# Moving nine weight sums behind the heads' scaling and the gating in VectorE's program (second layer of a fused block)

## The chip, the cores and the metric

The kernel runs on one core of a Trainium2 chip. The metric is the device time of one execution in microseconds (us), given as the median of several runs. Five engines take part: TensorE (PE in the profile; PEld is its loading of weights), VectorE (DVE), ScalarE (ACT), GpSimd (POOL) and SyncE (SP), which here only issues DMAs. Each works through its own program in order, and they wait for each other through semaphores.

## The reference, cut to what matters

The program is a stack of four layers. The one that is touched is the second, a neighbourhood attention over 512 tokens and 256 context tokens, with 32 heads of 64:

```
q, k, v, z = jnp.split(u @ w_in, 4, axis=-1)
q = rms_norm(q.reshape(bsz, n, NA_HEADS, NA_DH), qn_g)   # each head scaled by 1/rms
k = rms_norm(k.reshape(bsz, n, NA_HEADS, NA_DH), kn_g)
...
s = q_r . k_band * scale + bias, masked to the window;  s_ctx = q_r . k_ctx * scale
p = softmax(concat([s, s_ctx]))
o = p_band @ v_band + p_ctx @ v_ctx
out = (o * silu(z)) @ w_out                               # the gating
```

All is float32. The product `u @ w_in` is not computed as it stands, but by a scheme with seven products in the place of eight: the 1024 x 1024 piece of weights that belongs to one kind (k, q, v or z) of one group of heads is cut into quarters b11, b12, b21, b22, and the seven products use sums of quarters of the tokens and of the weights. The sums of the tokens exist once for the layer; the sums of the weights are made by VectorE for each piece ("chunk") anew, four of them, each a subtraction of 128 x 1024 elements:

```
t1 = b12 - b11      (n = 1)
t2 = b22 - t1       (n = 2)
t3 = b22 - b12      (n = 3)
t4 = t2 - b21       (n = 4)
```

## The kernel before, in words

The class `NearMixer` works on four groups of eight heads. The attention of a group is cut into 16 turns, one for a pair of heads and a quarter of the tokens. I number the turns of a group 0 to 15. Beside the attention of one group, TensorE computes the projections of the next group, so the turns of the groups 0, 1 and 2 carry projection products and the weight sums of the next group.

In a turn, TensorE does in this order: the scores (L1560, L1564, L1568), at times a transposition of freshly scaled heads (L1546), projection products (L1511, here four products of four matmuls; each matmul shows as two rows in the trace), the transposition of the softmax weights (L1577) ahead of the last three matmuls, and the attention's outputs (L1592). The products of a chunk come in the order `ORDER = (1, 2, 6, 5, 3, 7, 4)`; product 5 reads t1, product 6 reads t2, product 7 reads t3, product 4 reads t4. For the first step of a chunk TensorE waits for the sum with `pe.wait_ge(self.ts, 4 * b + {6: 2, 7: 3, 4: 4}[p])`. Before the outputs it waits for the gating of the turn before: `pe.wait_ge(self.gy, i)`.

VectorE's program of a turn, in `vector`, is: the maxima of the scores (L1826, L1834, L1839), the early parts (`add_parts`, which adds the products' results from PSUM, L1778 to L1795), the sums of squares of new heads (`sum_squares`, L1870), the softmax weights (`weights`, L1844, L1849, L1855), the held weight sums, the scaling of new heads (`evacuate`, L1881), the gating of the turn before (`gate`, L1863), and the late parts. GpSimd computes the factors 1/rms of the heads between the sums of squares and the scaling, with two small operations per tile of heads, an addition (L1702) and a power (L1704); the scaling waits for them.

A weight sum becomes due behind the part of a certain product. Where that part is an early one, most sums are not made at once but put into the list `self.held` and made later in the turn by `held_sums`; those that become due at a late part are made there. The weight sums are L1732 (t1), L1736 (t2), L1738 (t3) and L1742 (t4), all in `weight_sum`. SyncE loads the next quarters when the products and the third sum of the chunk before are done.

Of the kernel before, what the change touches and what calls it, by code (L numbers as in the profile page):

```python
# [1259 lines left out]
class NearMixer:  # L1260
# [557 lines left out]
    def vector(self, dve):  # L1818
# [3 lines left out]
        def maxima(i):  # L1822
            g, p, n = self.unit(i)
            dve.wait_ge(self.sc, 2 * i + 2)
            ctx = s.psS[:, 0:2, :].rearrange("p k (r x) -> p k r x", r=ROWS)[:, :, :, 0:32]
            nc.vector.tensor_reduce(self.m_ctx, ctx, mybir.AxisListType.XY, ALU.max).then_inc(self.cm, 1)  # L1826
            if n == 0:
                dve.wait_ge(self.bias_in[p], 64 * (g + 1))
            off = 16 - 16 * n + 8 * self.band[n]
            for k in range(2):  # L1830
                slot = s.bias[:, 2 * p + k, :]
                bias = bass.AP(slot.tensor, slot.offset + BANK - 1 - off, [slot.ap[0], [-64, ROWS], [-1, 32]])
                sc = self.scores_of(k)[:, :, 32:]
                nc.vector.tensor_tensor_reduce(  # L1834
                    out=sc, in0=sc, in1=bias, scale=1.0, scalar=-3.0e38, op0=ALU.add, op1=ALU.max,
                    accum_out=self.m_all[k]).then_inc(self.bi, 1)
                dve.wait_ge(self.bi, 2 * i + k + 1)
                dve.wait_ge(self.cm, i + 1)
                nc.vector.tensor_scalar(self.nm[i % 2][k], self.m_all[k], self.m_ctx[:, k:k + 1], -1.0, ALU.max,  # L1839
                                        ALU.mult).then_inc(self.mx, 1)  # L1840

        def weights(i):
            dve.wait_ge(self.ex, 2 * i + 2)
            nc.vector.reciprocal(self.rr, self.r[i % 2]).then_inc(self.rc, 1)  # L1844
            dve.wait_ge(self.rc, i + 1)
            n = self.unit(i)[2]
            if self.odd(n):
                for k in range(2):
                    nc.vector.tensor_scalar(s.e[:, k, BANK:], s.e[:, k, BANK // 2:BANK // 2 + DH], self.rr[:, k:k + 1], 0.5,  # L1849
                                            ALU.mult, ALU.mult).then_inc(self.tails, 1)  # L1850
            for k in range(2):
                e = s.e[:, k, 0:BANK]
                if self.odd(n):
                    dve.wait_ge(self.tails, 2 * self.odd_before(i) + k + 1)
                nc.vector.tensor_scalar(e, e, self.rr[:, k:k + 1], 0.5, ALU.mult, ALU.mult).then_inc(self.wt, 1)  # L1855

        def gate(i):
            g, p, n = self.unit(i)
            if n == 0:
                dve.wait_ge(self.zdone, 4 * g + (0, 2, 1, 3)[p] + 1)  # L1860
            dve.wait_ge(self.o, i + 1)
            cols = slice(n * P, (n + 1) * P)
            nc.vector.tensor_tensor(s.yT[:, g * 4 + p, cols], s.psO[:, 0:P], s.z[:, p, cols], ALU.mult).then_inc(self.gy, 1)  # L1863

        def sum_squares(g, kind, t, f):
            if kind == "z":
                return
            j = self.heads_index(g, kind, t)
            dve.wait_ge(self.sq, f + 1)
            nc.vector.reduce_sum(self.ss[:, j % 2, :], s.squares[f % 2].rearrange(view, h=HG), AX_X).then_inc(self.red, 1)  # L1870

        def evacuate(g, kind, t, f):
            if kind == "z":
                dve.wait_ge(self.sq, f + 1)
                z = s.z[:, t, :]
                nc.vector.scalar_tensor_tensor(z, s.squares[f % 2], 1.0, z, ALU.add, ALU.mult).then_inc(self.zdone, 1)
                return
            j = self.heads_index(g, kind, t)
            dve.wait_ge(self.rstd, j + 1)
            x = s.raw[:, j % 4, :].rearrange(view, h=HG)  # L1880
            nc.vector.tensor_tensor(x, x, spread(self.rs[:, j % 2, :], DH), ALU.mult).then_inc(self.evac, 1)  # L1881
# [8 lines left out]
        def out_part(q):  # L1890
            n, t = self.tiles[q]
            dve.wait_ge(self.pm, q + 1)
            if q == 0:
                dve.wait_ge(self.gate_in, 16)
                dve.wait_ge(self.old_in, 16 * LT)
            else:
                dve.wait_ge(self.pa, q)
            out_gate(s.psP[:, q % 4, :], n, t, self.pg, self.pa, q)
# [10 lines left out]
        def held_sums():  # L1909
            for b, n in self.held:  # L1910
                self.weight_sum(dve, b, n)
            self.held = []

        self.held = []
        for i in self.turns():
            lead = i + self.LEAD_TURNS
            if i >= 0:
                maxima(i)
            self.add_parts(dve, i, True)
            if i < 0:  # L1920
                held_sums()
            if lead in (1, 2):
                for t in range(2):
                    self.norm.vector_evacuate(dve, 2 * lead + t)
                self.norm.half_sums(dve, lead)
            for tile in self.finish[i]:
                sum_squares(*tile)
            if i >= 0:
                weights(i)
            if i >= 0:  # L1930
                held_sums()
            for tile in self.finish[i]:
                evacuate(*tile)
            if i >= 1:
                gate(i - 1)
            self.add_parts(dve, i, False)
            for q in self.out_ended(i - 1):
                out_part(q)
# [2165 lines left out]
```

## Time and profile before

| | us |
|---|---|
| median of 3 runs | 3019.38 (3019.23 to 3020.89) |
| the profiled execution | 3023.39 |
| span of its trace, first to last instruction | 3021.6 |
| PE busy in the span | 2917.1 (97%) |
| VectorE busy | 1500.2 (50%) |
| ScalarE busy | 796.2 (26%) |
| GpSimd busy | 456.1 (15%) |
| stretch of groups 0 to 2 (1440 to 1930 us): PE busy of 490.0 | 472.9 |
| the same stretch: VectorE busy | 306.9 |
| mean granted clock of TensorE | 0.986 of full speed |

Times in the trace are counted from the start of the span. In the timeline a row gives start, duration, engine, line, operation and what was idle just before it, with the instruction that ended the idle time. Instructions of one engine overlap a little at their ends, so that the next one on VectorE starts up to 0.1 us ahead of the end of the one before.

### The profile page before, as it was taken

The page shows a single profiled execution, that of the slowest core. Times are in us where ns is not written, and L with a number is a line of the kernel's source. Part 1 is how long each engine was busy: PE and PEld are TensorE (multiplying, and loading weights), DVE is VectorE, ACT ScalarE, POOL GpSimd, SP SyncE. Part 2 cuts the span into 40 slices and gives each one's busy share as a digit, 9 for nine tenths or more (in the row PEclk, how much of TensorE's full clock was granted, in tenths as well). Part 3 has the DMA queues.
Part 4 walks back from the last instruction along what each step waited for, and adds up shares of the span by engine and source line. Part 5 has one row for each costly group of instructions (what it writes and reads, how often), then busy time and mean ns, then how long its engine had stood idle before and what let it go on. Part 6 is the DMA issues. An engine that isn't in the chain of part 4 may idle for free. (4 is left out here: it accounts for less than half of the span.)

```text
span 3021.6 us, 38719 instructions
## 1 busy us (share of the span) xinstructions
PE 2917.1 (97%) x14883; PEld 1845.4 (61%) x14883; DVE 1500.2 (50%) x3557; ACT 796.2 (26%) x2061; POOL 456.1 (15%) x753
## 2 busy tenths in 40 slices
PE   5999999999999999999999999998999999999999
PEld 2435555555555554588787887753788887544454
DVE  2334545645545443646656666443455656344441
ACT  1113323323333322212323233221322222021230
POOL 0221321312213000120201112000001111011100
PEclk8999999999999999999999999999999999899999
DMA  7340000100012201321121211502421110040101
GB/s 252 118 160 30 29 28 29 56 28 29 29 40 86 97 1 25 124 72 50 49 78 43 71 50 50 181 1 70 127 57 29 29 57 29 1 140 3 56 1 56
DMA packets 137006, 185.65 MB, mean 61 GB/s; under 512 B 22236, under 2 KB 90364, under 8 KB 134772
## 3 DMA queue, kind: packets, MB, share of 16 engines
q1 hardware_dynamic: 135624, 183.09, 19.1%
q8 instruction: 119, 1.95, 0.3%
q14 instruction: 63, 0.52, 0.1%
q10 hardware_dynamic: 1200, 0.09, 0.0%
HBM read 173.49 MB, written 9.67 MB: 61 GB/s over the span
## 5 line engine op out<-in xcount | busy, mean ns | idle before, releaser
L493 PE MATMUL a_psP<-f_place,a_uT 128*128 128x512 f32 x768 | 351.0, 603 | 7.9 <-DMA f_place<-a_w_in 7.9
L493 PE MATMUL a_psP<-a_w,a_uT 128*128 128x512 f32 x768 | 349.2, 599 | 0.0
L753 DVE TENSOR_REDUCE a_small<-a_psS 128x1 f32<-128x768 f32 (+1 forms) x192 | 140.7, 774 | 401.8 <-PE a_psS L521 401.8
L493 PEld LDWEIGHTS a_psP<-f_place,a_uT 128*128 128x128 f32 x768 | 140.7, 192 | 167.3 <-issue 167.3
L493 PEld LDWEIGHTS a_psP<-a_w,a_uT 128*128 128x128 f32 x768 | 139.8, 191 | 158.0 <-issue 158.0
L1511 PE MATMUL b_psP<-n_body,b_uT 128*128 128x256 f32 x768 | 184.1, 382 | 1.3 <-DVE b_raw L1789 0.5
L648 ACT ACTIVATE a_e<-a_psS,a_small 128x768 f32<-128x768 f32 (+1 forms) x192 | 144.0, 754 | 139.0 <-DVE a_small L753 138.6
L1511 PEld LDWEIGHTS b_psP<-n_body,b_uT 128*128 128x128 f32 x768 | 142.8, 192 | 23.0 <-issue 2.8
L655 ACT COPY n_body<-a_psS 128x768 f32<-128x768 f32 (+1 forms) x96 | 63.1, 657 | 311.2 <-PE a_psS L530 311.2
L543 PEld LDWEIGHTS a_psO<-a_v,n_body 128*128 128x128 f32 x896 | 115.1, 192 | 45.9 <-issue 45.9
L1826 DVE TENSOR_REDUCE b_small<-b_psS 128x2 f32<-128x512 f32 x64 | 44.3, 691 | 189.0 <-PE b_psS L1568 189.0
L1663 ACT ACTIVATE n_body<-b_psS,b_small 128x512 f32<-128x512 f32 x128 | 86.8, 683 | 186.5 <-DVE b_small L1839 184.5
L2420 PE MATMUL d_ps<-d_uT,d_w 128*128 128x264 f32 x512 | 125.3, 395 | 0.0
L1670 ACT COPY n_body<-b_psS 128x512 f32<-128x512 f32 x128 | 68.7, 589 | 210.8 <-PE b_psS L1577 210.8
L1511 PE MATMUL b_psP<-b_wt,n_body 128*128 128x256 f32 x512 | 120.4, 382 | 3.1 <-DVE b_wt L1736 3.1
L521 PE MATMUL a_psS<-n_body 64*128 64x256 f32 (+1 forms) x640 | 122.4, 492 | 0.0
L2420 PE MATMUL d_ps<-d_uT,f_place 128*128 128x264 f32 x512 | 121.8, 389 | 0.0
L723 POOL TENSOR_TENSOR a_small<-a_small,a_eps_sum 128x1 f32<-128x1 f32 x96 | 18.3, 191 | 650.2 <-ACT n_body L659 650.2
L543 PE MATMUL a_psO<-a_v,n_body 128*128 128x128 f32 x896 | 115.5, 275 | 0.0
L1511 PEld LDWEIGHTS b_psP<-b_wt,n_body 128*128 128x128 f32 x512 | 95.0, 190 | 20.0 <-issue 5.6
L2420 PEld LDWEIGHTS d_ps<-d_uT,d_w 128*128 128x128 f32 x512 | 96.3, 195 | 15.3
L2420 PEld LDWEIGHTS d_ps<-d_uT,f_place 128*128 128x128 f32 x512 | 94.3, 190 | 15.3 <-issue 0.4
(495 smaller groups left out, 5182.8 us busy)
## 6 DMA issues: line engine op xcount, KB each, us to landing
n_body<-b_w_in SPq DMA_DIRECT2D x49, 512.0 KB, 3.7
f_place<-a_w_in SPq DMA_DIRECT2D x8, 2048.0 KB, 8.9
a_w<-a_w_in SPq DMA_DIRECT2D x8, 2048.0 KB, 9.0
a_yT<-mod_w SPq DMA_DIRECT2D x8, 1536.0 KB, 8.4
a_yT<-mod_w SPq DMA_DIRECT2D x8, 1024.0 KB, 17.8
f_place<-bias_table SPq DMA_DIRECT2D x64, 128.0 KB
f_place<-a_w_in SPq DMA_DIRECT2D x16, 512.0 KB, 6.9
d_w<-a_w_in SPq DMA_DIRECT2D x16, 512.0 KB, 6.9
```

Source lines behind the costliest of these rows:

```text
L493: ins = nc.tensor.matmul(s.psP[:, x % 2, :], s.uT[:, a, t * P:(t + 1) * P], w[:, a, :], start=(a == 0), stop=(a == KD - 1))
L521: ins = nc.tensor.matmul(self.score_banks(k, keys)[:, a:b], s.qT[rows, h, t * P:(t + 1) * P], s.kT[rows, g % 2, h, keys.start + a:keys.sta ...
L543: ins = nc.tensor.matmul(s.psO[:, 0:P], s.pT[:, k * P:(k + 1) * P], s.v[:, g % 2, keys.start // P + k, h * P:(h + 1) * P], start=(k == 0), ...
L648: nc.scalar.activation(s.e[:, k, 0:n], self.score_banks(k, keys), ACT.Exp, bias=self.nm[i % 2][:, k:k + 1], accum_out=self.r[i % 4][:, k:k ...
L655: nc.scalar.copy(s.pT[:, 0:n], self.score_banks(0, keys)).then_inc(self.wTr, 1)
L723: nc.gpsimd.tensor_tensor(self.c[b], self.oss[b], s.eps_sum[:, :], ALU.add).then_inc(self.order_o, 1)
L753: nc.vector.tensor_reduce(self.nm[i % 2][:, k:k + 1], self.score_banks(k, keys), AX_X, ALU.max, negate=True).then_inc(self.mx, 1)
L1511: ins = nc.tensor.matmul(out, lhsT, rhs, start=(a == 0), stop=(a == 3))
L1663: nc.scalar.activation(s.e[:, k, 0:BANK].rearrange("p (b r c) -> p r b c", b=8, c=8), s.psS[:, k, :].rearrange("p (r b c) -> p r b c", b=8 ...
L1670: nc.scalar.copy(s.e[:, k, 0:BANK], s.psS[:, k, :]).then_inc(self.wTr, 1)
L1826: nc.vector.tensor_reduce(self.m_ctx, ctx, mybir.AxisListType.XY, ALU.max).then_inc(self.cm, 1)
L2420: ins = nc.tensor.matmul(ps[:, 3 + x % 2, 0:n], s.w[h % 2][:, b, i, :], s.uT[:, b, half * n:(half + 1) * n], start=(b == 0), stop=(b == KD ...
```

## The change

`held_sums()` is called behind the gating and no longer ahead of the heads' scaling, for turns 0 and up. The turns ahead of the attention (`i < 0`) keep their own call.

```diff
@@ vector @@
                 sum_squares(*tile)
             if i >= 0:
                 weights(i)
-            if i >= 0:
-                held_sums()
             for tile in self.finish[i]:
                 evacuate(*tile)
             if i >= 1:
                 gate(i - 1)
+            if i >= 0:
+                held_sums()
             self.add_parts(dve, i, False)
```

A sum is held at this point in only three turns of a group, and in the groups 0, 1 and 2 alone: t4 of the q chunk in turn 8, t1 of the v chunk in turn 10, t3 of the v chunk in turn 11. Nine instructions move; all engines but VectorE keep their programs. All three turns also scale two tiles of heads.

VectorE, turn 8 of group 0 (L1855 the last of the softmax weights, L1742 the sum t4, L1881 the heads' scaling, L1863 the gating, L1789 the first late part), before with - and after with +:

```order
 L1849 TENSOR_SCALAR n_body<-n_body,b_small 128x64 x2
 L1855 TENSOR_SCALAR n_body<-n_body,b_small 128x512 x2
+L1881 TENSOR_TENSOR b_raw<-b_raw,b_small 128x512 x2
+L1863 TENSOR_TENSOR b_yT<-b_psO,b_z 128x128
 L1742 TENSOR_TENSOR b_wt<-b_wt,n_body 128x1024
-L1881 TENSOR_TENSOR b_raw<-b_raw,b_small 128x512 x2
-L1863 TENSOR_TENSOR b_yT<-b_psO,b_z 128x128
 L1789 TENSOR_TENSOR b_raw<-b_raw,b_psP 128x256
 L1791 TENSOR_TENSOR b_raw<-b_raw,b_psP 128x256
```

The sum t4 has moved past three instructions, two of which wait for GpSimd.

VectorE, turn 11 of group 0 (L1738 is the sum t3, L1783 a late part, behind which t4 of the same chunk, L1742, is made at once); turn 10 looks the same with L1732 (t1) in the sum's place:

```order
 L1849 TENSOR_SCALAR n_body<-n_body,b_small 128x64 x2
 L1855 TENSOR_SCALAR n_body<-n_body,b_small 128x512 x2
+L1881 TENSOR_TENSOR b_raw<-b_raw,b_small 128x512 x2
+L1863 TENSOR_TENSOR b_yT<-b_psO,b_z 128x128
 L1738 TENSOR_TENSOR n_body<-n_body,b_yT 128x4x256
-L1881 TENSOR_TENSOR b_raw<-b_raw,b_small 128x512 x2
-L1863 TENSOR_TENSOR b_yT<-b_psO,b_z 128x128
 L1783 TENSOR_TENSOR b_yT<-b_yT,b_psP 128x256
 L1742 TENSOR_TENSOR b_wt<-b_wt,n_body 128x1024
```

Here too the scaling and the gating now stand directly behind the softmax weights, and the sum ahead of the late parts.

## Rows read from the trace of the kernel before

**Rows 1.** The page, part 1: engine, busy us, share of the span, instructions.
```profile
PE 2917.1 (97%) x14883; PEld 1845.4 (61%) x14883; DVE 1500.2 (50%) x3557; ACT 796.2 (26%) x2061; POOL 456.1 (15%) x753
```

**Rows 2.** Waits of PE, 1440 to 1930 us: total us, times, longest.
```profile
PE b_psO L1592 <- DVE b_yT L1863: 13.1, 14, 1.9
PE b_psP L1511 <- DVE b_wt L1742: 4.0, 3, 1.3
```

**Rows 3.** Timeline of VectorE, turn 8 of group 0: start, us, instruction, idle before.
```profile
1459.80 0.88 DVE L1855 TENSOR_SCALAR n_body<-n_body,b_small 128x512 f32<-128x512 f32 x2
1460.59 1.22 DVE L1742 TENSOR_TENSOR b_wt<-b_wt,n_body 128x1024 f32<-128x1024 f32 x1
1461.72 0.69 DVE L1881 TENSOR_TENSOR b_raw<-b_raw,b_small 128x512 f32<-128x512 f32 x1
1464.22 0.69 DVE L1881 TENSOR_TENSOR b_raw<-b_raw,b_small 128x512 f32<-128x512 f32 x1 [1.81 <-POOL b_small L1704]
1464.83 0.28 DVE L1863 TENSOR_TENSOR b_yT<-b_psO,b_z 128x128 f32<-128x128 f32 x1
```

**Rows 4.** Timeline of PE, turn 8 of group 0.
```profile
1461.96 0.67 PE L1511 MATMUL b_psP<-b_wt,b_uT 128*128 128x256 f32 x2 [1.35 <-DVE b_wt L1742]
...
1465.17 1.09 PE L1592 MATMUL b_psO<-n_body,b_v 128*64 128x128 f32 x16 [0.37 <-DVE b_yT L1863]
```

**Rows 5.** Timeline of GpSimd, turn 8 of group 0: the second tile's addition.
```profile
1460.72 1.75 POOL L1702 TENSOR_TENSOR b_small<-b_small 128x8 f32<-128x8 f32 x1
```

**Rows 6.** Timeline of VectorE, turn 6 of group 1, which has no held sum.
```profile
1620.48 0.88 DVE L1855 TENSOR_SCALAR n_body<-n_body,b_small 128x512 f32<-128x512 f32 x2
1621.48 0.69 DVE L1881 TENSOR_TENSOR b_raw<-b_raw,b_small 128x512 f32<-128x512 f32 x1
1623.70 0.69 DVE L1881 TENSOR_TENSOR b_raw<-b_raw,b_small 128x512 f32<-128x512 f32 x1 [1.53 <-POOL b_small L1704]
```

**Rows 7.** Timeline of GpSimd, turn 6 of group 1: the second tile's addition.
```profile
1621.41 0.20 POOL L1702 TENSOR_TENSOR b_small<-b_small 128x8 f32<-128x8 f32 x1
```

**Rows 8.** Timeline of VectorE, turn 11 of group 0.
```profile
1490.41 0.69 DVE L1826 TENSOR_REDUCE b_small<-b_psS 128x2 f32<-128x512 f32 x1
...
1494.88 0.87 DVE L1855 TENSOR_SCALAR n_body<-n_body,b_small 128x512 f32<-128x512 f32 x2
...
1499.90 0.28 DVE L1863 TENSOR_TENSOR b_yT<-b_psO,b_z 128x128 f32<-128x128 f32 x1
```

**Rows 9.** Timeline of PE, end of turn 10 to end of turn 11, group 0.
```profile
1488.16 1.09 PE L1592 MATMUL b_psO<-n_body,b_v 128*64 128x128 f32 x16 [1.93 <-DVE b_yT L1863]
...
1492.49 1.67 PE L1511 MATMUL b_psP<-b_wt,n_body 128*128 128x256 f32 x7
...
1500.24 1.09 PE L1592 MATMUL b_psO<-n_body,b_v 128*64 128x128 f32 x16 [1.09 <-DVE b_yT L1863]
```

**Rows 10.** Timeline of PE, end of turn 10 and turn 11, group 1.
```profile
1670.66 1.30 PE L1592 MATMUL b_psO<-n_body,b_v 128*64 128x128 f32 x16 [1.92 <-DVE b_yT L1863]
...
1676.56 3.62 PE L1511 MATMUL b_psP<-b_wt,n_body 128*128 128x256 f32 x16
```

**Rows 11.** Timeline of VectorE, turn 11 of group 1.
```profile
1674.07 0.69 DVE L1826 TENSOR_REDUCE b_small<-b_psS 128x2 f32<-128x512 f32 x1 [1.15 <-PE b_psS L1568]
...
1678.81 0.87 DVE L1855 TENSOR_SCALAR n_body<-n_body,b_small 128x512 f32<-128x512 f32 x2
```

**Rows 12.** Timeline of VectorE, turn 11 of group 2.
```profile
1857.73 0.69 DVE L1826 TENSOR_REDUCE b_small<-b_psS 128x2 f32<-128x512 f32 x1 [0.88 <-PE b_psS L1568]
...
1862.80 0.87 DVE L1855 TENSOR_SCALAR n_body<-n_body,b_small 128x512 f32<-128x512 f32 x2
```

**Rows 13.** Stretches: length, busy us of PE to POOL, PE clock, DMA share, GB/s.
```profile
1673.00:1674.00 1.00, 1.00 (x7) 0.35 (x4) 0.00 (x0) 0.00 (x0) 0.00 (x0) 0.50 0.00 0
...
2682.50:2693.00 10.50, 10.03 (x44) 6.08 (x45) 7.62 (x27) 7.52 (x24) 3.73 (x8) 0.71 1.04 336
```

**Rows 14.** Timeline of PE in a later layer, after its longest wait there.
```profile
2682.53 1.03 PE L3339 MATMUL m_ps<-f_identity,m_tmp 16*128 16x16 f32 x8 [4.42 <-DVE m_tmp L3613]
```

## The prediction

> **What bounds the kernel now.** I first read the busy shares of the page: TensorE works through 97% of the span [rows 1]. So the time is TensorE's work plus its few waits, and a change in VectorE's order counts only through the waits that it shortens or lengthens. Next I read who waits for whom in the stretch of groups 0 to 2. TensorE waits there in 14 places for the gating, 13.1 us, and in 3 places for the sum t4, 4.0 us [rows 2]. Both kinds lie in the turns that the change touches, so I then read those turns instruction by instruction.
>
> In turn 8 VectorE makes t4 right behind the softmax weights, and TensorE stands idle for 1.35 us until it is there: its matmul starts at 1461.96, which is 1.37 us after t4 started at 1460.59 [rows 3, 4]. The three waits of this kind are alike, 4.0 us in three [rows 2]. At the end of this turn it waits 0.37 us more for the gating [rows 4]. In turn 10 it does not wait for t1, but 1.93 us for the gating; in turn 11 not for t3, but 1.09 us for the gating [rows 9]. The gating is late because the second tile's scaling waits 1.81 us for GpSimd [rows 3].
>
> **What the move gives: an earlier gating.** The trace has turns that scale two tiles of heads and hold no sum; they already have the order that the change makes. There the first scaling starts 1.00 us after the pair of L1855, and the second 2.22 us after the first [rows 6]. With a sum between, the first starts 1.92 us after L1855 and the second 2.50 us after that [rows 3]. So the second scaling stands 4.42 us behind L1855 with the sum and 3.22 us without, and the gating with it (0.61 us later in rows 3): 5.03 us become 3.83 us, 1.20 us earlier. That is nearly the whole sum, though VectorE waits for GpSimd in both orders, because GpSimd itself is faster without the sum: the second tile's addition takes 1.75 us beside the sum and the first scaling [rows 5], and 0.20 us where the sum is absent [rows 7].
>
> The Trainium skill, page "SBUF — State Buffer", section on the shared port pair, says why: a VectorE instruction with two SBUF inputs and a GpSimd instruction that reads SBUF exclude each other, and whichever starts first holds the pair to its end. By that rule the addition is blocked only by what VectorE runs at that moment, and moving the sum frees it; if the rule did not hold and the addition were slow by itself, the fourth case below would be the forecast. Rows 5 and 7 agree with the rule.
>
> The sum then runs behind the gating. It takes 1.13 us of VectorE's time (1460.59 to 1461.72 in rows 3), so what follows it starts 1.20 - 1.13 = 0.07 us earlier than now. The late parts are therefore not late.
>
> **What it costs: t4 in turn 8.** L1855 at 1459.80, first scaling 1460.80, second 1463.02, gating 1463.63, and t4 0.20 us behind the start of the gating (a 0.28 us instruction, and the next begins just ahead of its end) at 1463.83 in the place of 1460.59: 3.24 us later. TensorE's next matmul needs it, and behind this matmul in TensorE's order stand the transposition of the softmax weights, three more matmuls and the outputs. All start 3.24 us later; the 0.37 us wait for the gating at the end goes [rows 4]. Net 3.24 - 0.37 = 2.87 us later per place. Turn 9 has no wait of TensorE to take it up, so the whole of it counts. ScalarE's copies behind the transposition only shift along. Three places: +8.6 us.
>
> **The clock.** The wait in turn 8 grows from 1.35 to 1.35 + 3.24 = 4.59 us. After the 1.92 us wait of turn 10 in group 1 the granted clock fell to 0.50, the lower of the two levels, 1.2 GHz [rows 13]. From the outputs to the start of product 6 TensorE needed 5.90 us there [rows 10] and 4.33 us in group 0, where the clock stayed up [rows 9]: 1.57 us for one spell. Group 2 has a spell too: its way from the maxima to L1855 is 5.07 us [rows 12] against 4.47 in group 0 [rows 8]. So a wait of 1.9 us brings a spell twice in three times; the 1.35 us of turn 8 never does. At 4.59 us I expect a spell in all three places. Bounds from the rows: nothing below (if the spell lies within the wait), two spells, 3.2 us, above, since after the longest wait in a like situation, 4.42 us [rows 14], the clock was 0.71 over 10.5 us [rows 13], 6 us at the half. I take 1.6 us, one spell, the row of the 1.92 us wait being in the same stage and beside the same work. Three places: +4.8 us.
>
> The Trainium skill, page "TensorE: Matmul & The Clock Gate", part on the HAM clock gate, says that the chip's observation runs freely and does not start anew with a kernel. By that, equal waits end differently, and which of the three places gets a long or a short spell changes from run to run; rows 9 and 10, equal waits with different ends, agree. It alters no term, but it makes the sum good only to a spell or so.
>
> **What turns 10 and 11 give back.** In turn 10 nobody waits for t1: its only reader on TensorE, product 5, comes in turn 11, and t2 (L1736) follows it in VectorE's order anyway. The outputs start 1.20 us earlier, and the wait falls from 1.93 to 0.73 us, so I expect no clock spell behind it. What becomes of it depends on turn 11, whose gating sets the next outputs. In group 0 VectorE starts the maxima of turn 11 without any wait [rows 8], so earlier scores are no use to it; it gains 0.07 us. The way from the maxima to L1855 stays 4.47 us [rows 8], and the gating behind it comes 1.20 us earlier, since t3 moved. The outputs of turn 11 wait for the gating [rows 9], so TensorE is 1.27 us ahead at the end of both turns: the two gains do not add up.
>
> In group 1 the maxima waited 1.15 us for TensorE, slowed by the clock [rows 11]. That goes: 1.15 + 0.07 = 1.22 us. The way to L1855 was 4.74 us [rows 11] and falls to 4.47 us, 0.27 us; the gating gives 1.20 us. Sum 2.69 us. In group 2: 0.88 + 0.07, then 5.07 [rows 12] to 4.47 is 0.60, then 1.20: 2.75 us. Together 1.27 + 2.69 + 2.75 = 6.7 us.
>
> t3 itself ends some 3 us later in turn 11. Product 7, its first reader, comes in turn 12, behind outputs and scores. By my reckoning it is ready 1.4 us ahead of it (gating 1498.63, t3 from 1498.83, usable at 1500.20; product 7 not before 1501.6). t4 follows behind the late part as now. SyncE's load of the next b12 waits for t3 and is used only by the first sum of the next chunk, in a later turn. These cost nothing; if product 7 were caught it would be tenths of a us each.
>
> **Sum.** +8.6 + 4.8 - 6.7 = +6.7 us for the profiled execution of 3023.39 us, which is 4 us above the median; the terms are differences and hold for both. From 3019.38 that gives 3026.1 us. The clock's free phase makes the gain in turns 10 and 11 a little smaller or larger, as one, two or three of them had a spell.
>
> **The rivals.**
> One: the lower clock is not paid in turn 8 (spells fall within the wait). For it: the wait is itself long enough to cover much of a spell. Against: the 4.42 us wait of rows 14 did not hide its slow work [rows 13]. +8.6 - 6.7 = +1.9 us, 3021.3.
> Two: the clock stays low for two spells each. For it: rows 13 and 14. +8.6 + 9.6 - 6.7 = +11.5 us, 3030.9.
> Three, the other side: TensorE's wait in turn 8 is put down to t4, but really ends with something that does not move. It decides at the first matmul of product 4. Then only the earlier gating counts: -6.7 and 0.37 us in each of the three places, -7.8 us, 3011.6. Against: the three waits are as long as each other and end with t4 [rows 2, 4].
> Four: GpSimd's slow addition is not due to the sum. Then the second scaling stays at 3.42 us behind the first, the gating gains nothing (1464.83 in rows 3), t4 comes 4.44 us later, less 0.37, three times: +12.2 + 4.8 = +17.0 us, 3036.4. Against: rows 6 and 7.
>
> **How the numbers follow.** A measurement of this kernel can tell about 0.2%, 6.0 us, from no change. The forecast lies just beyond this bound, so its own chance splits. Forecast 0.52 (0.30 slower, 0.22 the same), one 0.22 (nearly all the same), two 0.16 (slower), three 0.05 (faster), four 0.05 (slower). Slower 0.52, the same 0.43, faster 0.05. The range goes from just below rival one to rival two: 3020 to 3031.
>
> **What would show it.** Right: in turn 8, L1881 directly behind L1855, the addition L1702 of the second tile at 0.20 us, and TensorE's wait for L1742 at 4.6 us in three places; the wait for the gating gone in turn 8, 0.7 us in turn 10, about 1.1 us in turn 11; the granted clock at 0.50 behind turn 8 and no longer in turn 11 of groups 1 and 2. Wrong: an addition that still takes 1.75 us, a wait for t4 that stays near 1.35 us, a new wait for L1738 at product 7, or full clock behind turn 8.

## The result and the profile after

The changed kernel takes 3027.51 us (median of 13 runs, 3022.86 to 3030.82) against 3019.38 us before (13 runs, 3018.11 to 3025.94). The ratio, estimated from all these runs, is 1.0021 with a 95% interval of 1.0012 to 1.0029 (the two medians alone would give 1.0027): slower by a fifth of a per cent. The profiled execution has a span of 3026.4 us in the place of 3021.6 us.

VectorE in turn 8 of group 0 after the change. It answers to [rows 3]:

```profile
1462.18 0.88 DVE L1855 TENSOR_SCALAR n_body<-n_body,b_small 128x512 f32<-128x512 f32 x2
1463.18 0.69 DVE L1881 TENSOR_TENSOR b_raw<-b_raw,b_small 128x512 f32<-128x512 f32 x1
1465.40 0.69 DVE L1881 TENSOR_TENSOR b_raw<-b_raw,b_small 128x512 f32<-128x512 f32 x1 [1.52 <-POOL b_small L1704]
1466.01 0.28 DVE L1863 TENSOR_TENSOR b_yT<-b_psO,b_z 128x128 f32<-128x128 f32 x1
1466.21 1.22 DVE L1742 TENSOR_TENSOR b_wt<-b_wt,n_body 128x1024 f32<-128x1024 f32 x1
```

From L1855 to the gating L1863 it is now 3.83 us (before 5.03), and to the sum t4, L1742, 4.03 us (before 0.79). GpSimd's two operations for the second tile in the same turn, the first of them answering to [rows 5]:

```profile
1463.11 0.20 POOL L1702 TENSOR_TENSOR b_small<-b_small 128x8 f32<-128x8 f32 x1
1463.39 1.98 POOL L1704 TENSOR_TENSOR b_small<-b_small 128x8 f32<-128x8 f32 x1
```

The addition fell from 1.75 to 0.20 us. TensorE in the same turn, the first row answering to the first of [rows 4], the last to its last:

```profile
1467.57 1.19 PE L1511 MATMUL b_psP<-b_wt,b_uT 128*128 128x256 f32 x2 [4.58 <-DVE b_wt L1742]
1468.56 1.91 PE L1577 MATMUL b_psS<-f_identity,n_body 128*128 128x128 f32 x8
1470.26 2.63 PE L1511 MATMUL b_psP<-b_wt,b_uT 128*128 128x256 f32 x6
1472.82 1.09 PE L1592 MATMUL b_psO<-n_body,b_v 128*64 128x128 f32 x16
```

The wait for t4 grew from 1.35 to 4.58 us, the wait for the gating at the end is gone, and the first two rows run at half speed and the third nearly so: two matmul rows take 1.19 us where they took 0.67. The granted clock of that stretch and of turn 11 of groups 1 and 2 (length, busy us by engine, PE clock in the third column from the right):

```profile
1467.00:1473.00 6.00, 5.43 (x20) 4.28 (x22) 1.42 (x4) 1.17 (x2) 0.00 (x0) 0.53 0.00 0
...
1680.00:1690.00 10.00, 9.99 (x71) 8.67 (x72) 9.04 (x22) 4.31 (x10) 3.01 (x4) 1.00 0.00 1
...
1866.00:1876.00 10.00, 9.44 (x68) 8.16 (x69) 9.57 (x24) 3.75 (x9) 2.45 (x4) 1.00 0.00 1
```

The low clock has moved (a stretch of it is called a spell): before it stood behind turn 10 and in turn 11 of groups 1 and 2 [rows 10, 13], now behind the wait of turn 8. How much of it there is differs from group to group. These are the 8.00 us that follow the wait in groups 0, 1 and 2:

```profile
1467.57:1475.57 8.00, 8.00 (x47) 6.26 (x48) 1.34 (x4) 1.17 (x2) 0.00 (x0) 0.68 0.01 2
1654.01:1662.01 8.00, 8.00 (x52) 6.59 (x53) 2.35 (x8) 2.03 (x4) 0.00 (x0) 0.82 0.01 2
1839.41:1847.41 8.00, 8.00 (x47) 6.15 (x48) 1.24 (x4) 1.17 (x2) 0.00 (x0) 0.67 0.01 2
```

TensorE is busy throughout, so what the clock takes there can be worked out: 8.00 x (1 - 0.68) = 2.6 us in group 0, 1.4 us in group 1 and 2.6 us in group 2. The spell of the kernel before, in the 8.00 us behind the wait of turn 10 in group 1 (1670.66 to 1678.66), shows 0.79, which is 1.7 us. In the 4.58 us of the wait itself the clock was 0.81, 0.95 and 0.83, but there it costs nothing. Wait and work together thus hold about twice as much of the low clock in groups 0 and 2 as in group 1 or in the old spell.

TensorE's waits in the stretch, answering to [rows 2]:

```profile
PE b_psP L1511 <- DVE b_wt L1742: 13.7, 3, 4.6
PE b_psO L1592 <- DVE b_yT L1863: 8.3, 11, 1.0
```

Three waits for the gating fewer (those of turn 8), 4.8 us less in all; the waits for t4 hold 9.7 us more.

To see place by place what a kernel loses, I compare the starts of the maxima (L1826) with those of the kernel before. They follow TensorE's scores, and between the touched turns the difference stays constant within 0.02 us, so each step in it belongs to a turn. In the table "turn 8" runs from the start of turn 8 to that of turn 10, and "turns 10 to 12" from there to the start of turn 13. In group 0, the kernel before starts turn 8, turn 10 and turn 13 here:

```profile
1455.31 0.69 DVE L1826 TENSOR_REDUCE b_small<-b_psS 128x2 f32<-128x512 f32 x1 [3.08 <-PE b_psS L1568]
...
1478.34 0.69 DVE L1826 TENSOR_REDUCE b_small<-b_psS 128x2 f32<-128x512 f32 x1 [4.76 <-PE b_psS L1568]
...
1512.97 0.69 DVE L1826 TENSOR_REDUCE b_small<-b_psS 128x2 f32<-128x512 f32 x1 [4.32 <-PE b_psS L1568]
```

and the changed kernel here:

```profile
1457.69 0.69 DVE L1826 TENSOR_REDUCE b_small<-b_psS 128x2 f32<-128x512 f32 x1 [3.07 <-PE b_psS L1568]
...
1485.99 0.69 DVE L1826 TENSOR_REDUCE b_small<-b_psS 128x2 f32<-128x512 f32 x1 [4.76 <-PE b_psS L1568]
...
1519.29 0.69 DVE L1826 TENSOR_REDUCE b_small<-b_psS 128x2 f32<-128x512 f32 x1 [4.32 <-PE b_psS L1568]
```

The lag is 2.38, 7.65 and 6.32 us: turn 8 adds 5.27, turns 10 to 12 take 1.33 back. The 2.38 us were there before the first touched instruction. The same reading for every kernel of this study, in us against the kernel before:

| kernel | turn 8, groups 0 / 1 / 2 | turns 10 to 12, groups 0 / 1 / 2 | whole stretch |
|---|---|---|---|
| changed | +5.27 / +4.22 / +5.38 | -1.33 / -2.76 / -2.81 | +7.97 |
| t4 ahead, t1 and t3 behind | 0 / 0 / 0 | -1.33 / -2.76 / -2.83 | -6.9 |
| t4 behind alone | +5.05 / +4.43 / +4.47 | +1.45 / -1.41 / -0.04 | +14.0 |
| changed, filled | +2.79 / +2.78 / +2.80 | -1.34 / -2.76 / -2.82 | +1.45 |
| before, filled | 0 / 0 / 0 | 0 / 0 / 0 | +0.1 |
| one SBUF input | 0 / 0 / 0 | -2.70 / -4.13 / -4.19 | -11.0 |
| gating first, t1 and t3 behind | -0.24 / -0.24 / -0.24 | -2.84 / -4.28 / -4.33 | -16.65 |
| gating first alone | -0.24 / -0.24 / -0.24 | -3.15 / -4.59 / -4.64 | -17.6 |

(The last two also gain in turns 5 to 7, some 1.5 us per group.) The touched stretch explains +7.97 us. The two spans differ by only 4.8 us; the other 3.2 us lie outside the stretch, where the change leaves all as it was. The traces place one step of 1.86 us in the changed kernel's favour: at the start of group 3 TensorE waits for a DMA in both kernels, and behind this wait the kernel before runs at half speed and the changed one does not (before, then after):

```profile
1948.07 2.08 PE L1526 MATMUL b_psP<-n_body,b_yT 128*128 128x512 f32 x2 [2.44 <-DMA n_body<-b_w_out]
```

```profile
1958.14 1.12 PE L1526 MATMUL b_psP<-n_body,b_yT 128*128 128x512 f32 x2 [2.17 <-DMA n_body<-b_w_out]
```

### The profile page after: what moved, and what is told of

Read it like the earlier page. It is cut to its first block and busy times, and to the rows that moved or that the text cites. A ratio compares the mean times of both kernels' runs of the same rounds, so it can differ in the third digit from the quotient of the medians.

```text
span 3026.4 us, 38719 instructions
## 1 busy us (share of the span) xinstructions
PE 2918.1 (96%) x14883; PEld 1846.0 (61%) x14883; DVE 1501.0 (50%) x3557; ACT 795.7 (26%) x2061; POOL 445.4 (15%) x753
## 5 line engine op out<-in xcount | busy, mean ns | idle before, releaser
L1826 DVE TENSOR_REDUCE b_small<-b_psS 128x2 f32<-128x512 f32 x64 | 44.2, 691 | 198.6 <-PE b_psS L1568 198.6
```

## The experiments

The ratios compare with runs of the kernel before that were made beside these: a median of 3019.81 us in 21 runs for most, of 3019.89 us in 7 runs for the two single runs and for the gating first alone.

**t4 stays ahead, t1 and t3 move.**

```diff
                 weights(i)
-            if i >= 0:
-                held_sums()
+            if i >= 0:
+                held_sums((4,))          # only a held t4
             for tile in self.finish[i]:
                 evacuate(*tile)
             if i >= 1:
                 gate(i - 1)
+            if i >= 0:
+                held_sums()              # the others
```

> Only the held sums t1 (turn 10) and t3 (turn 11) move behind the gating; t4 stays ahead of the scaling in turn 8. Theory (the loss of the change lies in turn 8 alone, the gain in turns 10 and 11): TensorE's wait for L1742 stays 1.35 us in three places with the clock up, the waits for the gating are 0.4, 0.7 and about 1.1 us; turns 10 and 11 together end about 1.3 us earlier in a group whose before had no clock spell there and about 2.8 us earlier where it had one, -4 to -8 us over three groups, so 3012 to 3015 us against 3019.4. Rival (t1 or t3 behind the gating costs something too, by product 7 waiting for t3 or the next loads): a wait for L1738 appears and the gain is under 2 us.

Measured: 3014.94 us (11 runs; ratio 0.9983, interval 0.9974 to 0.9992), faster than both kernels and within the 3012 to 3015 us expected. Its waits of TensorE in group 0, turns 8, 8, 10 and 11:

```profile
1462.38 0.67 PE L1511 MATMUL b_psP<-b_wt,b_uT 128*128 128x256 f32 x2 [1.34 <-DVE b_wt L1742]
1465.59 1.09 PE L1592 MATMUL b_psO<-n_body,b_v 128*64 128x128 f32 x16 [0.37 <-DVE b_yT L1863]
1487.39 1.09 PE L1592 MATMUL b_psO<-n_body,b_v 128*64 128x128 f32 x16 [0.72 <-DVE b_yT L1863]
1499.33 1.09 PE L1592 MATMUL b_psO<-n_body,b_v 128*64 128x128 f32 x16 [0.96 <-DVE b_yT L1863]
```

Turn 8 is as it was, turn 10's wait fell from 1.93 to 0.72 us, and turns 10 to 12 gain to 0.02 us what they gain in the changed kernel. No wait for t3 appears and the gain is more than 2 us, so the rival falls.

**t4 moves alone.** The same edit with `held_sums((1, 2, 3))` ahead of the scaling.

> Only the held sum t4 (turn 8) moves behind the gating; t1 and t3 stay ahead of the scaling. Theory: turn 8 is 4.2 to 5.4 us longer in each group, a wait of 4.6 us for L1742 and slow work behind it, +13 to +15 us in all, 3032 to 3034 us. Rival (what turn 8 loses is partly made up in the turns behind it, whatever their order): turns 10 and 11 shorter than in the kernel before by more than a clock spell, +8 us or less.

Measured: 3034.48 us (5 runs; ratio 1.0047, interval 1.0034 to 1.0059), half a microsecond above the expected range. Turn 8 costs 13.95 us in three groups, and both halves together, +14.0 - 6.9, are near the change's +7.97. Turns 10 and 11 have the old order here, and still they end 1.45 us later in group 0 and 1.41 us earlier in group 1. The wait is the old 1.93 us, but now the work behind it in group 0 is slow:

```profile
1490.95 1.56 PE L1592 MATMUL b_psO<-n_body,b_v 128*64 128x128 f32 x16 [1.93 <-DVE b_yT L1863]
1492.44 0.39 PE L1560 MATMUL b_psS<-b_mask_k,b_mask_q 64*128 64x256 bf16 x2
1492.63 1.06 PE L1564 MATMUL b_psS<-b_kT,b_qT 64*128 64x256 f32 x4
```

Before, the same wait at the same place passed without a spell [rows 9], and group 1 had one [rows 10]; here they have changed roles. So the length of the wait alone doesn't decide. The gain of turns 10 and 11 is 1.3 us in a group whose kernel before had no spell and some 2.8 us in one where it had, and how many of them had one is not fixed by the program as far as these runs show: the single runs of the kernel before have a mean granted clock between 0.984 (3026.2 us) and 0.989 (3017.45 us). Which places lose the clock in which run is not shown, as each kernel has one trace. (The control for the filling, below, is a second trace with the old order in turns 10 and 11, and its spells lie in groups 1 and 2 as before.)

Turn 8 repeats the pattern of the changed kernel. Behind the 4.58 us wait the clock is 0.71 over 8.00 us in group 0 and 0.79 in groups 1 and 2, which is 2.3, 1.7 and 1.7 us. So of six such places in two kernels three lost 1.4 to 1.7 us and three 2.3 to 2.6 us.

**The wait of turn 8 filled.**

```diff
+                if i % self.U == 8 and i < 3 * self.U:
+                    products(m0, m1 - 4)
+                    pe.wait_ge(self.ready, sum(at <= (i, 0) for at in self.heads))
+                    for _ in range(9):
+                        nc.tensor.matmul(s.psH[:, 0:256], s.ident[:, :], s.uT[:, 0, 0:256], start=True, stop=True)
+                    products(m1 - 4, m1 - tail)
```

> The changed kernel with nine matmuls without a use (into the idle PSUM tile of the heads, 128x256) put into TensorE's program of turn 8 ahead of product 4, so that it works while t4 is made. Theory (behind the 4.6 us wait some 1.4 to 2.6 us per place are lost to the lower clock): the wait for L1742 shrinks to 0.5 to 0.9 us, the clock stays up, and turn 8 is only about 2.8 us longer than before, so 4 to 7 us less than the changed kernel in three places, 3020 to 3023 us. Rival (the work behind the wait is slow for another reason, such as the transposition waiting for ScalarE): turn 8 stays 4.2 to 5.4 us longer, 3027.5 us or more.

Measured: 3025.25 us (11 runs; ratio to the kernel before 1.0014, interval 1.0005 to 1.0023), above the 3020 to 3023 us expected, while the trace shows what was expected. TensorE in turn 8 of group 0 (lines behind the inserted ones count seven higher: L1749 is t4):

```profile
1463.01 4.05 PE L1624 MATMUL b_psH<-b_uT,f_identity 128*128 128x256 f32 x18
1467.76 0.67 PE L1511 MATMUL b_psP<-b_wt,b_uT 128*128 128x256 f32 x2 [0.70 <-DVE b_wt L1749]
1468.27 1.04 PE L1577 MATMUL b_psS<-f_identity,n_body 128*128 128x128 f32 x8
1469.14 1.46 PE L1511 MATMUL b_psP<-b_wt,b_uT 128*128 128x256 f32 x6
1470.53 1.10 PE L1592 MATMUL b_psO<-n_body,b_v 128*64 128x128 f32 x16
```

The clock stays up, and turn 8 costs 2.78 to 2.80 us in each group. That is the part that the later t4 costs by itself; the rest of the change's 5.27, 4.22 and 5.38 us, 2.5, 1.4 and 2.6 us, is the clock's. It agrees with the 2.6, 1.4 and 2.6 us worked out above from the granted clock alone. The place-by-place reading shows 6.5 us less than the changed kernel, the medians 2.3 us less. Those are less sharp: single runs of one kernel lie up to 10 us apart (the kernel before, 3015.8 to 3026.2 in 21 runs), the trace's steps agree to hundredths.

**Control for the filling.** The kernel before with two such matmuls in the 1.35 us wait of turn 8.

> Control for the filled kernel: the kernel before with two matmuls without a use in turn 8 ahead of product 4, within its wait of 1.35 us. Theory (such matmuls cost nothing within a wait): the wait for L1742 falls to 0.4 to 0.5 us, and turn 8 ends where it did, within 0.1 us. Rival (they delay the work behind them): turn 8 longer by 0.2 us or more.

Measured: one run, 3014.24 us; by the trace turn 8 is unchanged within 0.02 us in all three groups. Its wait for t4 in group 0:

```profile
1462.44 0.67 PE L1511 MATMUL b_psP<-b_wt,b_uT 128*128 128x256 f32 x2 [0.48 <-DVE b_wt L1749]
```

1.35 us became 0.48 us and nothing moved. So the fillers cost nothing within this wait, and they gain nothing where no spell followed it. That its span is 9.1 us shorter than that of the kernel before (3012.5 and 3021.6) has other grounds: 1.8 us of it lie at the start of group 3 again, the rest is not placed.

**One SBUF input in the sum's place.**

```diff
         def held_sums():
             for b, n in self.held:
-                self.weight_sum(dve, b, n)
+                if n in (1, 3) and b % 4 == 2:
+                    ...
+                    source = self.quarter(b, 0)[2]
+                    nc.vector.tensor_reduce(self.m_ctx[:, 0:1], source, mybir.AxisListType.XY, ALU.max).then_inc(self.ts, 1)
+                else:
+                    self.weight_sum(dve, b, n)
```

> The order of the kernel before, but in turns 10 and 11 the held subtraction (two SBUF inputs, 1.22 us) is replaced by a maximum over one quarter of the weights (one SBUF input, 1024 elements, an estimate of 1.2 us by the length of the rows); t1 and t3 of the three v chunks are left uncomputed. Theory (GpSimd's addition is held up by VectorE instructions with two SBUF inputs, not by their being there): the second tile's L1702 falls from 1.75 to 0.20 us, the second scaling starts 1.5 to 2.3 us behind the first in place of 2.50, and the gating comes 0.8 to 1.5 us earlier though the same time of VectorE still stands ahead of it. Rival (the addition is slow because of the time at which it runs, whatever VectorE does): L1702 stays near 1.75 us and the gating where it was.

Measured: one run, 3006.61 us, of a kernel that leaves t1 and t3 of three chunks uncomputed; it is for the trace, not for the time. VectorE in turn 10 of group 0, and under it GpSimd:

```profile
1485.96 1.21 DVE L1916 TENSOR_REDUCE b_small<-n_body 128x1 f32<-128x1024 f32 x1
1487.09 0.68 DVE L1881 TENSOR_TENSOR b_raw<-b_raw,b_small 128x512 f32<-128x512 f32 x1
1488.05 0.69 DVE L1881 TENSOR_TENSOR b_raw<-b_raw,b_small 128x512 f32<-128x512 f32 x1 [0.27 <-POOL b_small L1704]
1488.66 0.28 DVE L1863 TENSOR_TENSOR b_yT<-b_psO,b_z 128x128 f32<-128x128 f32 x1
```

```profile
1486.10 0.20 POOL L1702 TENSOR_TENSOR b_small<-b_small 128x8 f32<-128x8 f32 x1
1486.38 1.64 POOL L1704 TENSOR_TENSOR b_small<-b_small 128x8 f32<-128x8 f32 x1
```

The instruction ahead of the scaling is as long as the sum (1.21 and 1.22 us), and yet GpSimd's addition takes 0.20 us. The second scaling follows the first after 0.96 us, sooner than the 1.5 us I had allowed. Against the 2.22 us of the changed kernel's turn 8, 0.92 us come from the power's start, 0.71 us ahead of the first scaling and not 0.21 us behind its start, and 0.34 us from its length, 1.64 us and not 1.98. The gating (1488.66) stands 3.49 us behind the start of L1855 (1485.17) in the place of 5.03: 1.54 us earlier, with an instruction of the same length still ahead of it. The theory stands: what delays GpSimd is the kind of the instruction, not the time.

The replacement differs from the sum in two things, though: it has one SBUF input, and it writes one column where the sum writes 1024. This run alone can't tell the two apart. A later layer of the kernel before can. There one and the same small operation of GpSimd (L2800) runs once beside an instruction of VectorE whose two wide inputs lie in SBUF, and once beside one with a wide input in SBUF and the other in PSUM. Both write hundreds of columns to SBUF; only the first holds GpSimd up, 0.73 us and not 0.19. VectorE's rows, then GpSimd's:

```profile
2287.72 0.77 DVE L2833 SCALAR_TENSOR_TENSOR d_ct<-d_zp,d_cw,d_ct 128x528 f32<-128x528 f32 x1
...
2295.11 0.42 DVE L2966 TENSOR_TENSOR d_X<-d_X,d_ps 128x256 f32<-128x256 f32 x1 [0.48 <-PE d_ps L2530]
```

```profile
2287.81 0.73 POOL L2800 TENSOR_TENSOR d_tiny<-d_tiny,d_fac 128x1 f32<-128x1 f32 x1
...
2295.12 0.19 POOL L2800 TENSOR_TENSOR d_tiny<-d_tiny,d_fac 128x1 f32<-128x1 f32 x1
```

The hold-up goes one way only in the rows read here. The first scaling, with two SBUF inputs, starts here while the power is running and still takes 0.68 us; in the kernel before the sum t4 starts at 1460.59, 0.17 us ahead of the end of the first tile's power, and takes its usual 1.22 us [rows 3].

**The gating first, t1 and t3 behind the scaling.**

```diff
                 weights(i)
+            first = i >= 1 and all(tile[1] != "z" for tile in self.finish[i])
+            if first:
+                gate(i - 1)
             if i >= 0:
-                held_sums()
+                held_sums((4,))
             for tile in self.finish[i]:
                 evacuate(*tile)
-            if i >= 1:
+            if i >= 1 and not first:
                 gate(i - 1)
+            if i >= 0:
+                held_sums()
```

> A version that may beat both: the gating of the turn before stands directly behind the softmax weights (in turns that finish no z), then the held t4, then the heads' scaling, then the held t1 and t3. Theory (TensorE waits for the gating only because the gating stands behind scalings that wait for GpSimd): all waits for the gating in turns with heads go, 13 us in the stretch of the three groups, less about 1.1 us per group in turn 11, where VectorE's maxima become the bound, plus the two spells of before: -11 to -16 us, 3004 to 3009 us. Rival (another wait takes their place: the scores then wait for ScalarE or the weights): half of it or less, 3012 us or more.

Measured: 3006.41 us (5 runs; ratio 0.9956, interval 0.9942 to 0.9969), as expected. TensorE no longer waits for the gating anywhere in the stretch.

**The gating first alone.** As above, but all held sums stay between the gating and the scaling.

> Only the gating moves, directly behind the softmax weights and ahead of the held sums, which stay ahead of the scaling (not in turns that finish z). Theory (the outputs wait for the gating alone, and the held sums need not move once it does not stand behind them): about the gain of the version with t1 and t3 behind the scaling, -12 to -17 us over the three groups, 3003 to 3008 us. Rival (t1 and t3 still delay the scaling, and with it the next scores or the maxima): 3 to 7 us less gain, 3009 to 3013 us.

Measured: 3005.10 us (4 runs; ratio 0.9951, interval 0.9934 to 0.9969). TensorE's waits in the stretch:

```profile
PE b_psP L1511 <- DVE b_wt L1742: 4.6, 3, 1.6
```

The gating's line is gone. VectorE in turn 10 of group 0:

```profile
1480.25 0.28 DVE L1863 TENSOR_TENSOR b_yT<-b_psO,b_z 128x128 f32<-128x128 f32 x1
1480.45 1.22 DVE L1732 TENSOR_TENSOR b_wt<-b_yT,n_body 128x1024 f32<-128x1024 f32 x1
1481.59 0.68 DVE L1881 TENSOR_TENSOR b_raw<-b_raw,b_small 128x512 f32<-128x512 f32 x1
1483.20 0.69 DVE L1881 TENSOR_TENSOR b_raw<-b_raw,b_small 128x512 f32<-128x512 f32 x1 [0.92 <-POOL b_small L1704]
```

The second scaling still waits 0.92 us for GpSimd, but nobody waits for the scaling. GpSimd's addition is fast here too, because it now falls beside the gating, which has one input in PSUM; the power behind it meets the sum and takes 2.50 us:

```profile
1480.38 0.20 POOL L1702 TENSOR_TENSOR b_small<-b_small 128x8 f32<-128x8 f32 x1
1480.66 2.50 POOL L1704 TENSOR_TENSOR b_small<-b_small 128x8 f32<-128x8 f32 x1
```

In its stretch this kernel is 0.9 us ahead of the version that also moves t1 and t3: once the gating stands first, moving the held sums is worth nothing more. By their medians the two can't be told apart.

## Why the prediction was right

The forecast was 3026.1 us, the measured 3027.51; where the sum says +6.7 us, the touched stretch shows +7.97. The mechanism is the one forecast, term by term. That the median comes as near as 1.4 us is partly luck: single runs of one kernel spread over 8 to 10 us. Point by point:

- The bound: right. No engine's work changed; all of the difference in the touched stretch is in TensorE's waits (+4.9 us) and its clock.
- The earlier gating: 3.83 us behind L1855, as forecast, and the addition at 0.20 us. That the sum blocks GpSimd, which I took from the Trainium skill (page "SBUF — State Buffer", section "Who interferes with whom") and two rows, is now shown by the one-input kernel and the rows beside it. By the same rule GpSimd, where it starts first, would hold up VectorE. The rows read here show no such hold-up: the scaling at 1487.09 took its usual 0.68 us beside a running power. The forecast did not use that half.
- t4 in turn 8: 2.87 us per place were forecast, 2.79 measured with the clock kept up. The 0.08 us are an overlap: without a wait the outputs start 0.07 us ahead of the end of the row before them (1470.53 against 1469.14 + 1.46), where I had taken off the 0.37 us wait alone.
- The clock behind turn 8: 1.6 us per place were forecast, 2.5, 1.4 and 2.6 us measured, 6.5 us in place of 4.8. This is the one term that was mis-sized. I took one spell of the old size for every place; group 1 had that (1.4 us), but groups 0 and 2 had about twice as much of the low clock, of which part fell into the wait and 2.5 and 2.6 us behind it. The bounds of 0 and 3.2 us held.
- Turns 10 and 11: -6.9 us measured, -6.7 forecast, with 1.33, 2.76 and 2.81 us in the groups against 1.27, 2.69 and 2.75. That the two turns' gains don't add up in group 0 is confirmed: in the changed kernel the maxima of turn 11 start at 1497.93 without a wait.
- t3 was ready for product 7, by the margin forecast: L1738 started at 1506.41, and product 7, at 1509.15, shows no wait.
- Of the rivals, the second (two spells everywhere) came true in kind in groups 0 and 2 and not in group 1, and at 2.5 us rather than 3.2, as part of the low clock fell into the wait; the first is refuted by the half speed behind the wait, the third by the wait of 4.58 us for t4, the fourth by the addition at 0.20 us.

Not settled: all of the 3.2 us outside the touched stretch. The changed kernel enters the stretch 2.38 us late, gains 1.86 us at the start of group 3, where it is spared a clock spell, and 3.7 us more by the end. Both traces have the same work there, and the granted clock differs (0.97 before and 0.99 after between 2200 and 2600 us), but for the 3.7 us no single place is shown.

## What to carry to other kernels

When a producer is moved in an in-order engine's program, sort its consumers: the sum that TensorE was already waiting for (t4) cost 2.8 us and 1.4 to 2.6 us of low clock in each place, the two that it wasn't waiting for cost nothing and gave 6.9 us. And move the late result itself before moving what stands in front of it: the gating, which waited for nothing, stood behind two scalings that waited for another engine, and putting it first was worth nearly 15 us by the medians where the best arrangement of the sums gave 5; some 4.5 us of that lie in turns 5 to 7, where no sum is held. A wait's price includes the clock behind it; a filled wait shows that part by itself.

## What the runs showed of the hardware that I had not expected

- The same 1.93 us wait at the same place passed at full clock in the kernel before [rows 9] and brought a spell with t4 moved alone (1.56 us for the outputs instead of 1.09). A gain that rests on a spell near that length can't be counted on per place.
- Nine matmuls without a use, 4.05 us of TensorE's time in a wait of 4.6 us, gained 1.4 to 2.6 us per place by keeping the clock up.
- The low clock reaches back into the wait, where it is free. Of six waits of 4.58 us in two kernels three cost 1.4 to 1.7 us behind them and three 2.3 to 2.6 us.
- A reduction of 1024 columns with one SBUF input left GpSimd's 128x8 addition at 0.20 us; a subtraction of the same length with two, and the scaling behind it, made it 1.75 us. The other way round no hold-up was seen: VectorE's scaling took 0.68 us beside a running GpSimd power.
